# Preparing the cross attention's key input two tiles at a time while the delta rule still runs

## The reference, cut to what matters

```
mem_n = rms_norm(mem, norm_mem_g)            # 256 x 2048
k, v  = split(mem_n @ w_kv, 2)               # keys and values, 2048 columns each
scores = q @ k^T / sqrt(512); p = softmax(scores); o = p @ v
```

## Time and profile before

| | |
|---|---|
| median of three runs | 2895.39 us (2895.37, 2895.39, 2898.47) |
| the profiled execution's own time | 2899.32 us |
| its span | 2897.5 us |
| PE busy | 2872.1 us, 99% |
| DVE busy | 1901.7 us, 66% |
| ACT busy | 1398.8 us, 48% |
| mean granted TensorE clock | 0.998 |

### The profile page before, as it was taken

How to read it: one execution, slowest core, us unless ns; L and a number is a source line. 1 busy time by engine, 2 the same in 40 slices (tenths; PEclk the granted TensorE clock), 3 DMA queues, 4 the chain that set the end, 5 groups by cost and what they waited for, 6 DMA issues and landing times.

```text
span 2897.5 us, 39222 instructions
## 1 busy us (share of the span) xinstructions
PE 2872.1 (99%) x16096; PEld 2494.7 (86%) x16096; DVE 1901.7 (66%) x2417; ACT 1398.8 (48%) x1792; POOL 56.7 (2%) x101
## 2 busy tenths in 40 slices
PE   9999999999999999999999999999999999999998
PEld 8899888888888888888888888888888888888886
DVE  7645557678665668778778765456666555656555
ACT  5434644356443445656655653434345434444444
POOL 0000210000000000000000000000000000000000
PEclk9999999999999999999999999999999999999999
DMA  7444445464554544343333345544354455554543
GB/s 275 184 181 160 146 160 200 178 247 168 197 188 176 210 149 160 131 146 131 140 137 131 133 173 189 190 179 163 138 203 175 184 193 192 190 200 177 193 182 145
DMA packets 73138, 506.80 MB, mean 175 GB/s; under 512 B 8416, under 2 KB 8544, under 8 KB 13184
## 3 DMA queue, kind: packets, MB, share of 16 engines
q1 hardware_dynamic: 71568, 498.21, 46.3%
q0 software_dynamic: 1104, 5.90, 0.6%
q10 hardware_dynamic: 288, 0.18, 0.0%
HBM read 500.07 MB, written 2.10 MB: 173 GB/s over the span
## 4 chain that ended last, share of the span: by engine, by line
PE 96%; DVE 1%; ACT 1%; DMA 1%; issue 0%; SPq 0%; ACTq 0%; POOL 0%; DVEq 0%
PE double L1283 87%; PE bank L1283 7%; PE bank L1286 2%; ACT whi L1659 0%; DMA vec<-in_vec 0%; DMA raw<-in_wall 0%; DVE wlo L2003 0%; DVE cacc L2009 0%; DVE acc L2003 0%; ACT L1694 0%; SPq L2776 0%; DMA mblk<-in_memT 0%; ACT AA L1798 0%; DVE rr L2003 0%; ACT L1855 0%
## 5 line engine op out<-in xcount | busy, mean ns | idle before, releaser
L1283 PE MATMUL double<-AA,whi 128*128 128x512 f32 (+1 forms) x5008 | 1657.6, 382 | 5.0 <-DVE wlo L2003 4.9
L1283 PE MATMUL double<-AA,wlo 128*128 128x256 f32 (+1 forms) x4624 | 1300.8, 281 | 0.0
L1659 ACT ACTIVATE whi<-raw 128x1024 fp32r<-128x1024 f32 x926 | 924.9, 1049 | 721.6 <-PE double L1283 691.8
L2003 DVE TENSOR_TENSOR wlo<-raw,whi 128x1024 fp32r<-128x1024 f32 (+1 forms) x934 | 1101.7, 1214 | 237.6 <-ACT whi L1659 235.0
L1283 PEld LDWEIGHTS double<-AA,whi 128*128 128x128 f32 x5008 | 916.1, 188 | 194.0 <-DVE wlo L2003 6.4
L1283 PEld LDWEIGHTS double<-AA,wlo 128*128 128x128 f32 x4624 | 871.4, 188 | 1.5
L1283 PE MATMUL double<-whi,AA 128*128 128x512 f32 x1536 | 489.2, 393 | 0.5 <-DVE wlo L2003 0.5
L1283 PEld LDWEIGHTS double<-whi,AA 128*128 128x128 f32 x1536 | 288.5, 188 | 60.7 <-DVE wlo L2003 1.3
L1283 PE MATMUL double<-whi,BB 128*128 128x512 f32 x1024 | 317.0, 389 | 0.0
L1283 PE MATMUL double<-wlo,AA 128*128 128x512 f32 x768 | 299.1, 389 | 0.0
L1283 PEld LDWEIGHTS double<-whi,BB 128*128 128x128 f32 x1024 | 192.2, 188 | 40.3
(11 more groups left out here) (333 smaller groups left out, 1849.7 us busy)
## 6 DMA issues: line engine op xcount, KB each, us to landing
raw<-in_wall SPq DMA_DIRECT2D x462, 1024.0 KB, 4.8
raw<-in_wall SPq DMA_DIRECT2D x9, 256.0 KB, 7.4
X<-in_xT SPq DMA_DIRECT2D x1, 2048.0 KB, 11.2
Mm<-in_memT POOLq DMA_DIRECT2D x1, 2048.0 KB, 15.4
tmp<-rqk POOLq DMA_DIRECT2D x16, 128.0 KB, 2.2
mblk<-in_memT SPq DMA_DIRECT2D x8, 256.0 KB, 4.4
out<-XT SPq DMA_DIRECT2D x8, 256.0 KB, 2.9
dec<-in_dec POOLq DMA_DIRECT2D x1, 1536.0 KB, 8.6
```

The lines of the kernel that those rows point to most:

```text
L1283: return q.matmul(out, lhsT, rhs, start=start, stop=stop, skip_group_check=True)
L1659: q.activation(whi[j % SPL][:, c], raw[j % RAW][:, c], ACT.Copy).then_inc(S("w_hi"), 1)
L2003: return q.tensor_tensor(out, a, b, o)
```

## The change

The first four blocks are loaded ahead of unit u+2 in place of the first two. Tiles 0 and 1 are made ready ahead of the second half of unit u+2, tiles 2 and 3 ahead of unit u+3 (where tiles 0 to 3 stood), tiles 4 and 5 ahead of the second half of u+3, tiles 6 and 7 behind it. Tiles 8 to 15 and the loads of blocks 4 to 7 keep their places.

```
             def loads():
-                for n in range(2):
+                for n in range(4):
                     add("load_mb", n)
...
+            def some(a):
+                return lambda: memn((a, a + 1), u + 2)
+
-            first_mem = {(u + 2, 0): loads, (u + 3, 0): lambda: memn(range(4), u + 3)}
+            first_mem = {(u + 2, 0): loads, (u + 2, 1): some(0), (u + 3, 0): some(2), (u + 3, 1): some(4)}
         pair("N", "gtb", phase3, ev_gtb_all, half=True, lazy=h == 7, hooks=first_mem if h == 7 else {})
-    for n in range(2, 8):
+    for n in range(4, 8):
         add("load_mb", n)
-    memn(range(4, 8), done["unit"])
+    memn((6, 7), done["unit"])
```

## The result

Over 20 runs each the kernel before took 2896.76 us (median) and the changed one 2900.47 us. The ratio is 1.0015, with a 95% interval of 1.0009 to 1.0021, which is 2.6 to 6.1 us more. The forecast was 2898.4 with a range of 2895.9 to 2901.8. So the time lies inside that range, but above the forecast's own narrow one (2897.3 to 2899.4) and among the times of its rival, the longer price. The profiled execution took 2899.58 us, span 2897.8.

The account below looks back on a forecast made before the run. PE, 96% of the chain that ended last, was taken as the bound. 4.25 us of delay less 1.7 of clock gives 2.55, plus 0.4 makes 3.0; on 2895.39 that is 2898.4 us, range 2895.9 to 2901.8.

Parts of the forecast that it names:

- the longer price: Rival, chance 0.30: both low stretches stay (2900.0 us) or block 0 lands late (2901.2); range 2899.5 to 2902.
- the credit of the clock: Behind PE's second `Tc,Mn`: its hole shrinks to 0.7 us, so the low stretch there goes, giving back 1.7 us.
- The wait at the head of two queues: On ACT and DVE, tiles 0 and 1 wait for block 0 ahead of the inverse's first step; `Tc` 4.6 us later.
- The 0.4 us that I added for company: Block 0's landing: 0.4 us more than its 5.1, for two more 256 KB transfers issued right behind blocks 0 and 1.
- The hole that is there: PE's 2.04 us idle ahead of the second `Tc,Mn`, behind block 5's landing: its cause stays, it shifts with the stretch.
- low stretch: Time after a PE hole with the granted clock near 0.50 (1.2 GHz, not 2.4); reckoned to lose 1.7 us.
- Not slower: Rival, chance 0.10: block 0 lands 2.9 us behind its issue, and the time stays at 2895.3 us.

Follow-up runs that it names:

- early_blocks: Changed kernel with blocks 0 and 1 loaded one unit earlier, order of DVE, ACT and PE kept; ratio to the kernel before 1.0005.
- late_block0: Changed kernel with its four loads issued in the order 2, 3, 0, 1; ratio to the kernel before 1.0023.
- loads_only: Kernel before with the first four blocks loaded together, tiles made ready where they were; ratio to the kernel before 1.0004.
- pairs_from_2: Changed kernel with tiles 0 and 1 put back ahead of unit u+3, the rest as changed; ratio to the kernel before 1.0001.
- after: The changed kernel, first profile; stretch 29.60 us, ratio to the kernel before 1.0015.
- after_again: The changed kernel profiled once more, unchanged, one execution; stretch 29.51 us.
- fix_on_after: Changed kernel with tiles 10 and 11 made ready later, together with tiles 12 to 15; ratio to the kernel before 1.0009.
- tiles_only: Changed kernel with only blocks 0 and 1 loaded ahead of unit u+2, tiles still two at a time; ratio to the kernel before 1.0033.
- fix_on_before: Kernel before with tiles 10 and 11 made ready later, together with tiles 12 to 15; ratio to the kernel before 0.9994.
- before: The kernel without the change, in the profile the prediction was made from; stretch 26.64 us, median time 2896.76 us.

## Why the prediction was right, and where it was off

The mechanism was right, and one term of the sum, the credit of the clock, was mis-sized. Against the mark `bank<-con,Mn` the steps can be laid beside the two profiles.

| step | forecast | measured |
|---|---|---|
| block 0, from issue to landing | 5.5 us | 5.40 |
| `Tc` on DVE | 5.0 later | 4.89 (1.61 to 6.50 behind the mark) |
| PE's `Tc,Mn` | 1.25 later | 1.15, hole 0.99 |
| PE's `Cm,Tn` | 4.25 later, hole 2.7 | 4.16, hole 2.52 |
| PE's second `Tc,Mn` | 4.65 later, hole 0.7 | 4.31, hole 0.58 |
| end of the stretch | 2.95 later | 2.96 |

**The wait at the head of two queues** was right in place and size, and the experiments show it alone to be the cause. It goes with the block's landing (early_blocks), it grows one for one with it (late_block0), it doesn't come from the shared start of the transfers (loads_only), nor from the other tiles (pairs_from_2). The 0.4 us that I added for company was a fair middle: with four loads together block 0 took 5.4, 5.5 and 5.9 us in after, after_again and fix_on_after, and 5.8 and 5.7 in loads_only and pairs_from_2; with two it took 5.0 in tiles_only (1664.03 to 1669.07), 5.1 to 5.2 in the kernel before and 5.3 in fix_on_before.

**The hole that is there** shifts and isn't mended. This was right, and fix_on_before shows that about half of it hung on tiles 10 and 11 (2.04 to 2.13 us with them, 1.00 without).

**The credit of the clock** was mis-sized, and it is why 3.0 us were forecast where 3.7 (by the medians) or 4.3 (by the ratio) were measured. The mechanism is there: a low stretch in front of a wait on something else is absorbed, as the hole of 0.58 us shows and the 6.46 us from `Cm,Tn` to the second `Tc,Mn`. But I subtracted a full 1.7 us for the low stretch that the kernel before had in its one profile, as if each execution had it. Among its three profiles one had it. Their mean stretch is (26.64 + 25.39 + 25.37) / 3 = 25.80, that of the changed kernel (29.60 + 29.51) / 2 = 29.56. The difference is 3.8 us, within the measured 2.6 to 6.1. Against the two without the low stretch it is 4.2. So the credit was worth 0.4 us on average and not 1.7. One profile could not size this term. It was too large even for that profile, where the low stretch cost 1.33 us. That the end of the stretch came out at 2.96 against 2.95 is partly luck: the second `Tc,Mn` was put 0.34 us too late (4.65 against 4.31), and the part behind it was credited with 1.7 us where it became 1.35 shorter (9.41 to 8.06).

**The base.** The forecast started from a median of three, 2895.39. Over 20 runs it is 2896.76, so 1.4 of the 2.1 us between forecast and result are the base, and the other 0.7 go to the credit, as far as the scatter lets one tell.

**The rivals.** Not slower: block 0 would have had to land 2.9 us after its issue. In every profile with the issue at its old place it took 5 us or more. The Trainium skill (DMA: Bandwidth & Descriptors, Queues, rings and completion order) says that completion is not first in, first out per issuing engine, and gives as its case a later transfer on one DMA engine and an earlier one on all sixteen. In no profile here did block 0 overtake: the `raw` load issued 0.4 us ahead of it landed 4.7 to 5.0 us after its own issue, before the block each time. The longer price is not what happened: no profile of the changed kernel has two low stretches or a block 0 that late, and its 2900.0 lies near the measured time only because the base and the credit were off. Its late landing came true in late_block0, by design. The first hole was 2.39 us where 2.4 were forecast, with a low stretch of its own. PE came to the second `Tc,Mn` 5.84 us later than before, as the rival's 5.85 has it, but the stretch grew by 4.5 us over the 26.64, since no low stretch stood behind that step.

## What to carry to other kernels

Where work waits for a transfer, as tiles 0 and 1 did here, putting it earlier in the queue of an engine doesn't make it earlier: its transfer has to be issued earlier, or else all that is queued behind it inherits the wait. In a chain that hops between engines, look for the place where it has slack (here 0.75 us ahead of `Cm,Tn`) and spend only that. And a clock that fell in one profile is a chance, not a constant: take two or three profiles before its cost goes into a sum.

## What the runs showed of the hardware

- Whether the clock falls behind a hole of 2 us differs from one execution to the next. Behind seven holes of 2.04 to 2.22 us in this stretch it fell twice. It fell behind both holes of 2.52 us, in the last 0.3 us of the one of 2.39 (late_block0), 3.6 us into the one of 6.85 (tiles_only), and behind one of 1.48 us (fix_on_after), but not behind one of 1.51 (tiles_only). Behind the holes of 1.00 (fix_on_before) and 1.28 us it stayed up.
- By the missing clock (PE's busy time by the missing share) a low stretch took 1.7 us in before, after, after_again, loads_only and fix_on_after, 1.8 in tiles_only and 3.3 in late_block0; in the last two the clock was low for 6.8 us. By the same instructions at both levels, one of the short ones cost 1.33 us (9.41 against 8.08 us), and next to nothing where PE met a wait behind it (6.46 and 6.22 us in the changed kernel from `Cm,Tn` to the second `Tc,Mn`, against 6.31 to 6.39 before).
- A 256 KB load issued 0.4 us behind a 1 MB load on SP's queue took 5.0 to 5.3 us to land with one more of 256 KB behind it, and 5.4 to 5.9 us with three more; the 1 MB load took 4.7 to 5.0, and block 5, issued 14 us and more behind block 0, took 2.7 to 3.1 in the ten profiles whose chain of waits shows it.
